# Six of the eight FFN input row blocks transposed by VectorE and DRAM instead of TensorE, and another order at the entry of the pool layer

## The reference, cut to what matters

```python
mix = jnp.concatenate([mla_out, mlstm_out], axis=-1) @ w_out[i]
h = h + rms_norm(mix, attn_post_norm[i])
f = rms_norm(h, ffn_pre_norm[i])
f = (jax.nn.silu(f @ w_gate[i]) * (f @ w_up[i])) @ w_down[i]
...
h = x @ w_in                       # pool_mixer
u, z = h[..., :D_POOL], h[..., D_POOL:]
csum = jnp.cumsum(u, axis=1)
...
outs.append((c - lag) / cnt - u[:, :, g])
```

## Time and profile before

| what | value |
|---|---|
| median of 3 runs | 1797.96 us (1797.88 to 1798.27) |
| the profiled execution's own time | 1797.84 us |
| its span in the profile | 1796.0 us |
| PE busy | 1777.2 us, 99% of the span |
| DVE busy | 1410.6 us, 79% |
| POOL busy | 1102.2 us, 61% |
| ACT busy | 690.0 us, 38% |
| granted TensorE clock | 0.999 of full |

### The profile page before, as it was taken

How to read it: one execution, slowest core, us unless ns; L and a number is a source line. 1 busy time by engine, 2 the same in 40 slices (tenths; PEclk the granted TensorE clock), 3 DMA queues, 4 the chain that set the end, 5 groups by cost and what they waited for, 6 DMA issues and landing times.

```text
span 1796.0 us, 22436 instructions
## 1 busy us (share of the span) xinstructions
PE 1777.2 (99%) x8398; PEld 1485.6 (83%) x8398; DVE 1410.6 (79%) x1665; ACT 690.0 (38%) x1211; POOL 1102.2 (61%) x772
## 2 busy tenths in 40 slices
PE   9999999999999999999999999999999999999998
PEld 8888888888888888888888888887788888888886
DVE  7889877766696658666599989679888875798896
ACT  6555577843431111111233334414433343333314
POOL 4066632360399979888778778633655465567554
PEclk9999999999999999999999999999999999999999
DMA  7342410032303323233375631133232231943232
GB/s 210 95 154 57 126 34 17 22 125 94 128 27 103 129 71 118 96 116 117 106 281 179 231 129 48 48 98 90 94 123 100 106 141 71 366 173 107 73 102 94
DMA packets 142718, 206.53 MB, mean 115 GB/s; under 512 B 48897, under 2 KB 104833, under 8 KB 138897
## 3 DMA queue, kind: packets, MB, share of 16 engines
q1 hardware_dynamic: 142434, 205.03, 34.0%
q10 hardware_dynamic: 176, 0.07, 0.0%
HBM read 151.51 MB, written 53.04 MB: 114 GB/s over the span
## 4 chain that ended last, share of the span: by engine, by line
PE 77%; DVE 1%; ACT 1%; issue 0%; POOL 0%; DVEq 0%; ACTq 0%
PE ps L1392 68%; PE ps L1744 2%; PE ps L1746 2%; PE ps L1745 2%; PE ps L1978 1%; PE ps L1977 1%; PE ps L1979 1%; PE ps L1865 0%; ACT xs_hi L2553 0%; PE ps L1645 0%; PE ps L1731 0%; PE ps L1620 0%; PE ps L1635 0%; DVE xs_lo L3489 0%; POOL ring_lo L1327 0%
## 5 line engine op out<-in xcount | busy, mean ns | idle before, releaser
L1392 PE MATMUL ps<-f_hi,ring_hi 128*128 128x512 f32 x368 | 143.5, 390 | 0.0
L1392 PE MATMUL ps<-f_lo,ring_hi 128*128 128x512 f32 x368 | 143.3, 389 | 0.0
L1392 PE MATMUL ps<-f_hi,ring_lo 128*128 128x512 f32 x368 | 143.3, 389 | 0.0
L1238 POOL TENSOR_TENSOR ring_lo<-w_sum,ring_hi 128x512 fp32r<-128x512 f32 x84 | 128.4, 1529 | 7.0
L1392 PE MATMUL ps<-d_w_hi,d_hid_hi 128*128 128x512 f32 x312 | 121.6, 390 | 0.0
L2427 ACT ACTIVATE f_copy<-ps 128x512 f32<-128x512 f32 x63 | 37.3, 596 | 219.4 <-PE ps L1392 211.6
L1392 PE MATMUL ps<-d_w_hi,d_hid_lo 128*128 128x512 f32 x312 | 121.5, 389 | 0.0
L1392 PE MATMUL ps<-d_w_lo,d_hid_hi 128*128 128x512 f32 x312 | 121.5, 389 | 0.0
L1392 PE MATMUL ps<-f_low,ring_hi 128*128 128x512 f32 x336 | 117.2, 389 | 0.0
L1327 POOL TENSOR_TENSOR ring_lo<-w_sum,ring_hi 128x512 fp32r<-128x512 f32 x56 | 87.6, 1574 | 40.7 <-ACT ring_hi L2548 40.6
L1237 POOL TENSOR_SCALAR ring_hi<-w_sum 128x512 fp32r<-128x512 f32 x84 | 79.1, 942 | 31.3 <-PE ps L1392 30.2
(11 more groups left out here) (574 smaller groups left out, 5859.8 us busy)
## 6 DMA issues: line engine op xcount, KB each, us to landing
d_raw<-hid_rows SPq DMA_DIRECT2D x37, 512.0 KB, 4.4
stage<-in_w_up SPq DMA_DIRECT2D x22, 512.0 KB, 4.6
wd_raw<-in_w_down SPq DMA_DIRECT2D x22, 512.0 KB, 5.0
raw_w<-in_w_gate SPq DMA_DIRECT2D x20, 512.0 KB, 4.9
stage<-in_pool_w_in SPq DMA_DIRECT2D x16, 512.0 KB, 4.9
raw_w<-in_pool_w_in SPq DMA_DIRECT2D x16, 512.0 KB, 4.7
m_rows<-u_row SPq DMA_DIRECT2D x16, 512.0 KB, 2.6
z_rows<-z_buf SPq DMA_DIRECT2D x8, 1024.0 KB, 4.1
```

What stands on the lines that cost most here:

```text
L1238: g.tensor_tensor(view(lo), src, view(hi).bitcast(F32), ALU.subtract).then_inc(w_split, 1)
L1392: last = mm(out_ap, l, r, start=(start and j == 0), stop=(stop and j == n - 1), skip_group_check=onto)
```

## The change

1. FFN input blocks 0 to 5 (`TURNED = 6`): DVE turns `f_blk` in 32x32 blocks into `f_turned` (two buffers), directly after it wrote it. SP, after the spill and the load of x of the same block, waits for that, issues four stores to DRAM (one for each 32 partitions; 128-byte runs, 1,024 in each store), waits until all four have landed, and issues one load (512-byte runs) that puts the block into `f_full`. ACT then only makes the high part from `f_full`, and DVE splits from `f_full`. Both do it one block later than before (`take_f(t - 2)`, `split_f(t - 2)` in the chain of block `t`). Blocks 6 and 7 still go through TensorE; the place of `f_transposed(6)` and `f_transposed(7)` and what they wait for is unchanged.
2. Pool entry, PE: in the first quad the high part of product 2 comes before product 4, its low part after.
3. Pool entry, ACT: all four parts of `x_sum_hi(0)` before the first copy; one part of `x_sum_hi(1)`, the second copy, then the other three; in the second quad the first copy waits for DVE's first sum only (not the second), and the second and third copies come before three of the weight splits.
4. Pool entry, DVE: for the first pair, `window_rows(0, 1)` moves from before the second quad's sums to before their last two; in the other pairs the wait for `m_stored` moves behind the first sum.

```diff
+        f_turned = [at(f"f_turned{i}", [P, D], Z + 4 * KB * i) for i in range(2)]
...
+        f_dram = nc.dram_tensor("f_blocks", [2, D, P], F32, kind="Internal").ap()
...
+        TURNED = 6
+        MOVED = TURNED // 2 * 16 * 5
+        def moved(t):
+            return 16 * 5 * (t // 2 + 1)
...
# SP, in the loop over t
                 if t + 1 < TB:
                     sp.dma_start(x_blk[:], a["x_lanes"][(t + 1) * P:(t + 2) * P, :]).then_inc(xblk_in, 16)
+                if t < TURNED:
+                    sp.wait_ge(xr_ready, t + 1)
+                    blocks = f_dram[t % 2].rearrange("(j c) (b r) -> b c j r", c=32, b=4)
+                    for b in range(4):
+                        turned = f_turned[t % 2][32 * b:32 * b + 32, :].rearrange("c (j r) -> c j r", r=32)
+                        sp.dma_start(blocks[b], turned, **SMALL).then_inc(xr_stored[t % 2], 16)
+                    sp.wait_ge(xr_stored[t % 2], moved(t) - 16)
+                    sp.dma_start(f_full[:, :, t * P:(t + 1) * P],
+                                 f_dram[t % 2].rearrange("(k p) n -> p k n", p=P)).then_inc(xr_stored[t % 2], 16)
# PE
             for t in range(2, TB):
                 pe.wait_ge(mix_taken, t - 1)
                 mixed(t, 0)
-                if t == 2:
-                    f_transposed(0)
                 mixed(t, 1)
-                f_transposed(t - 1)
+                if t > TURNED:
+                    f_transposed(t - 1)
...
-            quad(N_QUADS, 0, x_factors, (0, 4), x_sums)
-            sum_product(2, 2)
+            quad(N_QUADS, 0, x_factors, (0,), x_sums)
+            sum_high(2, 2)
+            quad(N_QUADS, 0, x_factors, (4,), x_sums, at=1)
+            sum_low(2)
# ACT
             def take_f(t):
                 for j in range(2):
+                    if t < TURNED:
+                        act.wait_ge(xr_stored[t % 2], moved(t))
+                        f(f_part[j][t // 4][0][:, :, (t % 4) * P:(t % 4 + 1) * P],
+                          f_full[:, 4 * j:4 * j + 4, t * P:(t + 1) * P], ACT.Copy).then_inc(rows_hi, 2)
+                        continue
...
-                if t >= 1:
+                if 1 <= t <= TURNED:
+                    act.wait_ge(xr_ready, t)
+                elif t:
                     act.wait_ge(rows_full, 16 + 2 * t)
...
-                if t >= 1:
-                    take_f(t - 1)
+                if t >= 2:
+                    take_f(t - 2)
+            take_f(TB - 2)
             take_f(TB - 1)
...
-            x_sum_hi(0, (0, 1, 2))
+            x_sum_hi(0)
             act.wait_ge(w_split, IN_BLOCKS + blocks_split(N_QUADS) + 7)
             copy_product(N_QUADS, 0, 0)
-            x_sum_hi(0, (3,))
             x3_part(15)
-            x_sum_hi(1)
+            x_sum_hi(1, (0,))
             copy_product(N_QUADS, 0, 1)
+            x_sum_hi(1, (1, 2, 3))
...
-                act.wait_ge(quad_summed, IN_SUMS + 4 * q + 2)
+                act.wait_ge(quad_summed, IN_SUMS + 4 * q + (2 if i else 1))
                 copy_product(q + 1, 4, 0)
...
+                if i == 0:
+                    next_hi(q + 1, 0)
+                    act.wait_ge(quad_summed, IN_SUMS + 4 * q + 2)
+                    copy_product(q + 1, 4, 1)
+                    copy_product(q + 1, 4, 2)
+                    next_hi(q + 1, 1, 2, 3)
# DVE, chain of block t
                 v.scalar_tensor_tensor(f_blk[:], h1_blk[:], stat_f[:, t:t + 1], ffn_gain[:],
                                        ALU.mult, ALU.mult).then_inc(rows_ready, 1)
-                if t >= 1:
-                    split_f(t - 1)
+                if t < TURNED:
+                    dve.wait_ge(rows_ready, 8 + t + 1)
+                    if t >= 2:
+                        dve.wait_ge(xr_stored[t % 2], moved(t - 2))
+                    v.transpose(f_turned[t % 2][:], f_blk[:]).then_inc(xr_ready, 1)
+                if t >= 2:
+                    split_f(t - 2)
+            split_f(TB - 2)
             split_f(TB - 1)
...
                 window_rows(i, 0)
-                window_rows(i, 1)
                 if i:
+                    window_rows(i, 1)
                     dve.wait_ge(z_stored, 16 * i)
                 quad_sums(q + 1, 4, x_copy, [z_buf[:, b, :] for b in range(4)],
-                          first_rows_lo if i == 7 else lambda: pool_sums(2 * i + 3))
+                          first_rows_lo if i == 7 else lambda: pool_sums(2 * i + 3),
+                          low=None if i else lambda: window_rows(0, 1))
```

More of the change, by code:

```diff
@@ L979, in x3_store @@
             def x3_store(i, n):
-                sp.wait_ge(xr_ready, 4 * i + 2 * n + 2)
+                sp.wait_ge(xr_ready, TURNED + 4 * i + 2 * n + 2)
                 for b in range(4):
@@ L1032, in sp_program @@
             for n in range(2):
-                sp.wait_ge(xr_stored[n], 64 * 4)
+                sp.wait_ge(xr_stored[n], MOVED + 64 * 4)
             for b in range(4):
@@ L1732, in f_transposed @@
                     if k % 4 == 3:
-                        last.then_inc(rows_full, 1)
+                        last.then_inc(rows_full, 2 * TURNED + 1 if t == TURNED and k == 3 else 1)
             def mixed(t, e):
@@ L1905, in pe_program, with sum_high @@
             sum_of = {2: 0, 1: 1, 3: 2, 6: 3}
-            def sum_product(o, at):
+            def sum_high(o, at):
                 i = sum_of[o]
@@ L1913, in sum_product @@
                 pe.wait_ge(xs_hi_ready, 4 * i + 4)
-                (w_h, w_l), (x_h, x_l) = ring[o], x_sum[i]
+                (w_h, w_l), x_h = ring[o], x_sum[i][0]
                 dst = ps[:, bank_of[o], :]
@@ L1919, in sum_product, with sum_low @@
                     mm(dst, w_l[:, cs], x_h[:, k, :], start=False, stop=False, skip_group_check=(o >= 4))
+            def sum_low(o):
+                i = sum_of[o]
                 pe.wait_ge(xs_split, i + 1)
                 for k in range(4):
-                    last = mm(dst, w_h[:, k * P:(k + 1) * P], x_l[:, k, :], start=False, stop=(k == 3),
-                              skip_group_check=(o >= 4))
+                    last = mm(ps[:, bank_of[o], :], ring[o][0][:, k * P:(k + 1) * P], x_sum[i][1][:, k, :], start=False,
+                              stop=(k == 3), skip_group_check=(o >= 4))
                 last.then_inc(prod_full, 1)
+            def sum_product(o, at):
+                sum_high(o, at)
+                sum_low(o)
             def x_sums(o):
@@ L2594, in first_block_rows @@
                 if i == 0:
-                    act.wait_ge(xr_stored[1], 64 * 4)
+                    act.wait_ge(xr_stored[1], MOVED + 64 * 4)
                 else:
@@ L2626, in act_program @@
                     next_hi(q, 4, 5, 6)
-                act.wait_ge(quad_summed, IN_SUMS + 4 * q + 2)
+                act.wait_ge(quad_summed, IN_SUMS + 4 * q + (2 if i else 1))
                 copy_product(q + 1, 4, 0)
[L2629 to L2633, removed]
+                if i == 0:
[4 more added lines that the diff above has]
+                    next_hi(q + 1, 1, 2, 3)
+                else:
+                    next_hi(q + 1, 0, 1)
+                    copy_product(q + 1, 4, 1)
+                    next_hi(q + 1, 2)
+                    copy_product(q + 1, 4, 2)
+                    next_hi(q + 1, 3)
                 if i == 7:
@@ L3181, in split_f @@
                     f_h, f_l = f_part[j][t // 4]
-                    v.tensor_tensor(f_l[:, :, ts], ps[:, 4 + 2 * (t % 2) + j, :].rearrange("p (k n) -> p k n", k=4),
-                                    f_h[:, :, ts].bitcast(F32), ALU.subtract).then_inc(rows_split, 1)
+                    src = ps[:, 4 + 2 * (t % 2) + j, :].rearrange("p (k n) -> p k n", k=4)
+                    if t < TURNED:
+                        src = f_full[:, 4 * j:4 * j + 4, t * P:(t + 1) * P]
+                    v.tensor_tensor(f_l[:, :, ts], src, f_h[:, :, ts].bitcast(F32), ALU.subtract).then_inc(rows_split, 1)
             split_mix(0, 1)
@@ L3459, in x3_turned @@
                 if i:
-                    dve.wait_ge(xr_stored[n], 64 * i)
+                    dve.wait_ge(xr_stored[n], MOVED + 64 * i)
                 turned = x_turned[n][:].rearrange("p (t m c) -> p m t c", m=2, c=32)[:, j % 2]
@@ L3519, in dve_program @@
                 x_sums(3, k)
-            dve.wait_ge(xr_stored[0], 64 * 4)
+            dve.wait_ge(xr_stored[0], MOVED + 64 * 4)
             second_sums((2,))
@@ L3527, in pool_sums @@
                 block_sums(N_QUADS + q, w_sum[q % 2], 3 - q % 2)
-            dve.wait_ge(xr_ready, 16)
-            dve.wait_ge(xr_stored[1], 64 * 4)
+            dve.wait_ge(xr_ready, TURNED + 16)
+            dve.wait_ge(xr_stored[1], MOVED + 64 * 4)
             for c in range(2):
@@ L3557, in dve_program, with rows_stored @@
                 q = N_QUADS + 2 * i
-                if i:
+                def rows_stored():
                     for c in range(2):
                         dve.wait_ge(m_stored[c], 16 * i)
```

(3 more changed lines are left out.)

## The result

The changed kernel takes 1802.88 us (median of 14 executions, 1799.99 to 1804.43), the kernel before 1797.86 in the same job (1797.73 to 1799.22): ratio 1.0026, 95% interval 1.0018 to 1.0033. It is slower, by 5.0 us. I had forecast 1793.6 with a range to 1800.3: wrong in size and in sign. The profiled execution is the fastest of the 14 (1799.99, span 1798.2).

What follows compares the result with a forecast made beforehand. PE, busy 99% of the span, bounds the kernel. FFN part -5.5 + 1.3 + 0.5 = -3.7 us, with 0.8 from the pool entry: 4.5 off 1797.84; with 0.12 and 0.2 added, 1793.6 us, range 1791.8 to 1800.3.

Steps and rivals of the forecast that it cites:

- What leaves PE: FFN blocks: six blocks' transposes leave PE, 0.92 us each, for -5.5 us.
- The wait for the split of block t-2: FFN blocks: block 7's transposes still wait for block 5's split, now behind f_blk, for +1.3 us.
- a sign of being wrong: Profile after: waits of PE inside the FFN loop, or no wait in quad 3, would show the prediction wrong.
- DVE and the transpose: FFN blocks: DVE's 128x1024 transpose takes about 1.4 us; DVE has 1.9 us of room, nothing on PE's path.
- The ring: SP's DMA round: D 4.1 us, round 10.4 against PE's 10.88; block 2 2.9 us late, each later round gaining 0.5.
- the term of 0.5: FFN block 7: lateness left from SP's rounds, which PE pays there, +0.5 us.
- the balance rival: FFN ring: D from 4.5 to 5.0, block 7 2.8 to 5.8 late, part 1 -1.4 to +1.6; chance 0.22.
- the slow ring: FFN ring slower than PE: at D = 5.4 block 7's chain 8.3 us late, time 1801.3; chance 0.15.
- The entry's first products: Pool entry: waits on copies shrink or go; PE at the end of quad 2 3.7 us earlier, product 4 some 4.
- The pool entry: Quad 3: DVE starts about 0.8 us earlier and sets product 5's copy, so only 0.8 us is gained.
- 0 if POOL's overlap slows DVE more: Pool entry: lower bound on the 0.8 us gain; the upper was 3.7.
- PE now waits about 3 us in one place: Pool entry: PE's new wait of about 3 us before product 5 of quad 3.

Runs made afterwards that it cites:

- e6: e3 with SP issuing each load into f_full only after the next block's spill and x load: 1793.74 us, ratio 0.9977 to the kernel before.
- e3: e2 without PE's wait, before the transposes of blocks 6 and 7, for the splits of blocks 4 and 5: 1796.39 us.
- e1: The kernel before with only the pool-entry parts (2 to 4) of the change: 1802.21 us, ratio 1.0021.
- e4: e1 with DVE's window_rows(0, 1) back at its old place, ahead of the second quad's sums: 1799.49 us.
- e8: e1 with twelve low-by-low matmuls that nothing needs, put on PE just ahead of its long wait at the pool entry: 1799.91 us.
- e2: The kernel before with only the FFN part (1) of the change: 1799.44 us, ratio 1.0007.
- e12: The changed kernel run again, no edit: 1802.37 us, ratio 1.0025 to the kernel before.
- e11: e4 with ACT making all four parts of x_sum_hi(1) before the second copy, as before the change: 1798.63 us.
- e9: e4 with ACT, first pair only, making two product copies and two high parts before its two silus, not behind them: 1799.54 us.

## Why the prediction was wrong, point by point

**What leaves PE: right.** The forecast was -5.5 us. In e6 block 6 is turned at 475.70, before at 481.17, 5.5 earlier.

**The wait for the split of block t-2: half seen.** I gave it one term, +1.3 us for block 7. It has two places: block 6's transposes wait in the same way for block 4's split (1.4 us), which I did not list. It stands inside the loop, which the prediction gave as a sign of being wrong. And I priced the split at 1.28 us from the earlier trace rows, where one operand comes from PSUM. Now both lie in SBUF (`f_full` and `f_hi`), and with POOL at work it takes 2.8 (with POOL only starting, in e6 at 482.87, 1.29). e3 measures the two together: 3.05 us by the medians, 2.6 at block 7 by the profiles, where I had 1.3. The change had also made the wait needless, and I took that it stays for a fact of the kernel.

**DVE and the transpose: right.** 1.25 us for 128x1024 (1.4 foreseen), hidden.

**The ring: mechanism right, size short.** From SP's first stores to its load took 414.05 to 419.17, 5.1 us (5.5 foreseen). The round took (472.18 - 419.17) / 5 = 10.6 (10.4 foreseen), as later stores share the queue with the x load and took 5.6 to 7.5. Block 2's chain was 425.02 - 421.53 = 3.5 us late (2.9), block 7's 2.1 (0.5): each round gave back 0.3, not 0.5. So the term of 0.5 was 2.1 (2.6 in e3, whose chain starts at 478.50), and e6 removes it by order alone. That lies between the forecast and the balance rival (2.8 to 5.8), far from the slow ring's 8.3; that the part costs +1.5, near the balance rival's upper end of +1.6, comes from other terms.

**The entry's first products: right in kind, too large.** Product 4 of the third quad starts at 1285.44 in e1, before at 1288.13: 2.7 us earlier, where I had about 4.

**The pool entry: this step failed.** "DVE starts about 0.8 us earlier". It came 0.7 later at the two sums in e4 (1287.57 against 1286.83) and 1.8 later with the moved windows. I had seen that DVE sets that moment, but took DVE's durations from before. Two things were missed: the new ACT order makes DVE 0.9 us late at 1243 (I had a wait of 0.5, more than made up by an earlier PE; at the operation of 1252.89 DVE is 0.65 late in e1, not 0.8 early), and DVE's operations on two SBUF operands take about twice as long beside POOL, which both the shift and the moved windows bring about (1.1 us each). The earlier trace rows and the bound "0 if POOL's overlap slows DVE more" had the mechanism, but not a loss. The Trainium skill, "SBUF — State Buffer", SBUF: two separate sides, says that a DVE operation with two SBUF inputs and a GpSimd operation that reads SBUF take one shared pair of ports in turn, the later one being blocked until the other is done. The traces agree: 2.33 us for the first sum of the moved window beside POOL (e1), 1.23 for the same sum without (e4).

**What PE's wait costs: missing altogether, the second step that failed.** I named the wait ("PE now waits about 3 us in one place"; it was 4.8) and gave it no price beyond its length. e8 prices the fall of the clock behind it at 2.3 us by the medians, 2.0 by the rows of e1 and e8. The same fall behind the FFN wait costs 1.6. No rival held it either. In the profiled executions of the two parts alone, 3.7 us over the forecast are the clock, 2.6 are DVE (1.8 late for 0.8 early), and 3.5 are the splits and the late chain of block 7.

The sum again, by rows: the pool part is 1.8 late plus 2.1 of slow clock, 3.9. The FFN part is 5.5 gained, 2.6 lost to the splits (e2 against e3), 2.7 to the late chain of block 7 (e3 against e6) and 1.6 to the slow clock, 1.4. That is +5.3; the profiled executions of the two parts give +5.4, their medians +5.7, and the two medians of both parts together +5.0 and +4.4. In e12's profile (+5.0) the stretch up to the pool entry is 1.7 late, DVE adds 1.6 and the slow clock behind product 5 another 1.6, where e1 had 1.8 and 2.1.

## What to carry to other kernels

In the pool entry PE's waits were set by another engine's pace, and the new orders moved them but did not remove them. Four waits of about one microsecond were cheaper than one of nearly five, because the clock fell behind the long one and what followed ran slowly. So before an order is tightened, ask where PE meets the slow engine next and how long it will stand there; if it must stand, matmuls put there can pay, even useless ones, as in e8. And when a stage leaves a resource (a bank, a place in a queue), its old waits and its place in the order must be looked at again: the same FFN change costs 1.5 us as written and gives 4.1 without one dead wait and with one load issued later.

## What the runs showed of the hardware

- The granted clock went from 1.00 to 0.50 behind or shortly after waits of 2.7 us (e11), 2.8 (e3), 3.2 (e9), 3.8 (e2) and 4.8 (e1); in e1 it fell before PE started again, in e2 during the transposes, in e11 only after six matmuls. It was back at full speed behind ten matmuls in e1, behind eight transposes and six matmuls in e2. Behind waits of 3.17 (e4) and 3.25 (the first profile after) it stayed at 1.00 in the profiled execution. In one kernel the clock falls in some executions and not in others (at block 7 in e12, not in the first profile after). The times of the changed kernel spread by 4 us, those of e6, without a long wait, by 0.5. Even e8, with its wait of 2.1, has five of eleven executions 1.1 us or more above the rest. Why the clock falls in one execution and not in another is open here.
- A 128x512 subtraction on DVE with both operands in SBUF took 1.4 us beside POOL (two in 2.77 us at 484.94), 0.64 with one operand in PSUM beside POOL (two in 1.27 at 487.62 of the same profile) and 0.64 with both in SBUF and POOL only starting (e6 at 482.87).
- 4,096 packets of 128 bytes, stored with nothing behind them, took about 5.1 us from issue to the next load (414.05 to 419.17), 5.6 to 7.5 with other transfers on the queue. The estimate from packets of 4 and 256 bytes was 5.5.
